# The first three weight chunks as plain fp32 products, issued between the modulation sums

## The reference, cut to what matters

```python
c_act = jax.nn.silu(c)
mod = (c_act @ w_ada[l] + b_ada[l])[:, None, :]
sh1, sc1, g1, sh2, sc2, g2 = jnp.split(mod, 6, axis=-1)
h = _rmsnorm(x, norm_g[l, 0]) * (1.0 + sc1) + sh1
...
z = h @ w_in            # qa, ka, va, qb, kb, vb, fb, qc, kc, vc, qi, ki, wi, zg
...
qc_r = _rope(heads(qc, C_HEADS), cos, sin)
kc_r = _rope(kc[:, :, None, :], cos, sin)[:, :, 0, :]
qi_r = _rope(heads(qi, IDX_HEADS), cos, sin) * (IDX_DIM ** -0.5)
ki_r = _rope(ki[:, :, None, :], cos, sin)[:, :, 0, :]
```

## Time and profile before

| | |
|---|---|
| median of 3 runs | 810.53 us (810.25 to 810.9) |
| the profiled execution's own time | 810.55 us |
| its span, first to last instruction | 808.8 us |
| mean granted TensorE clock | 0.972 of full speed |
| TensorE busy | 752.6 us, 93% |
| VectorE busy | 538.7 us, 67% |
| ScalarE busy | 397.1 us, 49% |
| GpSimd busy | 108.3 us, 13% |

### The profile page before, as it was taken

How to read it: one execution, slowest core, us unless ns; L and a number is a source line. 1 busy time by engine, 2 the same in 40 slices (tenths; PEclk the granted TensorE clock), 3 DMA queues, 4 the chain that set the end, 5 groups by cost and what they waited for, 6 DMA issues and landing times. The chain is left out here.

```text
span 808.8 us, 14361 instructions
## 1 busy us (share of the span) xinstructions
PE 752.6 (93%) x6052; PEld 734.9 (91%) x6052; DVE 538.7 (67%) x776; ACT 397.1 (49%) x540; POOL 108.3 (13%) x91
## 2 busy tenths in 40 slices
PE   2499999999897999999999999999999999999995
PEld 2499999999896999999999999999989999999994
DVE  4968988666856677777746456926675556566554
ACT  3175555555424554444443337618445565655533
POOL 0020000000500100000000060000005754342000
PEclk9699999999998999999999999969999999999998
DMA  9965555655345165545565614523335644334001
GB/s 353 415 237 194 222 207 216 245 203 214 115 145 220 53 209 208 185 181 186 202 244 202 213 56 168 201 101 103 122 141 184 207 171 157 105 105 158 1 1 53
DMA packets 20952, 139.57 MB, mean 173 GB/s; under 512 B 2356, under 2 KB 2996, under 8 KB 5016
## 3 DMA queue, kind: packets, MB, share of 16 engines
q1 hardware_dynamic: 20600, 137.80, 47.2%
q0 software_dynamic: 288, 0.85, 0.3%
HBM read 137.59 MB, written 1.05 MB: 171 GB/s over the span
## 5 line engine op out<-in xcount | busy, mean ns | idle before, releaser
L941 DVE TENSOR_TENSOR wlo<-raw,whi 128x2048 fp32r<-128x2048 f32 (+1 forms) x106 | 239.1, 2257 | 156.8 <-ACT whi L584 152.2
L1463 PE MATMUL res<-hhi,whi 128*128 128x256 f32 (+1 forms) x1168 | 337.1, 289 | 6.3 <-DVE hlo L977 4.2
L1464 PE MATMUL res<-hhi,wlo 128*128 128x256 f32 (+1 forms) x1168 | 331.3, 284 | 0.0
L1465 PE MATMUL res<-hlo,whi 128*128 128x256 f32 (+1 forms) x1168 | 331.3, 284 | 0.0
L584 ACT ACTIVATE whi<-raw 128x2048 fp32r<-128x2048 f32 (+1 forms) x106 | 197.7, 1867 | 154.1 <-issue 115.7
L1463 PEld LDWEIGHTS res<-hhi,whi 128*128 128x128 f32 (+1 forms) x1168 | 223.6, 191 | 8.6 <-issue 3.8
L1464 PEld LDWEIGHTS res<-hhi,wlo 128*128 128x128 f32 (+1 forms) x1168 | 223.6, 191 | 0.3
L1465 PEld LDWEIGHTS res<-hlo,whi 128*128 128x128 f32 (+1 forms) x1168 | 223.4, 191 | 0.2
L1463 PE MATMUL res<-uhi,whi 128*128 128x256 f32 x176 | 50.0, 284 | 1.0 <-ACT y L778 1.0
L1464 PE MATMUL res<-uhi,wlo 128*128 128x256 f32 x176 | 49.4, 281 | 0.0
L1465 PE MATMUL res<-ulo,whi 128*128 128x256 f32 x176 | 49.4, 281 | 0.0
(11 more groups left out here) (293 smaller groups left out, 1164.9 us busy)
## 6 DMA issues: line engine op xcount, KB each, us to landing
raw<-in_wts SPq DMA_DIRECT2D x100, 1024.0 KB, 5.0
raw<-in_w_ada SPq DMA_DIRECT2D x16, 1024.0 KB, 6.1
gates<-in_w_ada SPq DMA_DIRECT2D x6, 1024.0 KB, 8.2
raw<-in_wts SPq DMA_DIRECT2D x4, 768.0 KB, 7.6
y<-in_w_ada SPq DMA_DIRECT2D x2, 1024.0 KB, 10.7
x<-in_xT SPq DMA_DIRECT2D x2, 512.0 KB, 6.3
outT<-x SPq DMA_DIRECT2D x4, 256.0 KB, 2.4
biasA<-in_relb SPq DMA_DIRECT2D x1, 768.0 KB
```

Of the source, the lines that this page charges most:

```text
L941: nc.vector.tensor_tensor(wlo[c % SPL][:, 0:b], raw[RAW_OF["w", c] % RAW][:, 0:b], whi[c % SPL][:, 0:b].bitcast(f32), ALU.subtract).then_i ...
L1463: mm(out, ah, bh, start=first, stop=False)
L1464: mm(out, al, bh, start=False, stop=False)
L1465: return mm(out, ah, bl, start=False, stop=last)
```

## The change

The chunks 0 to 2 (`DIRECT = 3`) are no longer split. They are loaded whole into the place of `gates`, and `direct(c, j)` multiplies them in fp32 by the tiles `tb`, two input tiles (a pair j) at a time, four matmuls a call. The modulation blocks lie in three new shared buffers and `y`. ScalarE makes `tb` (scale and shift in one instruction) from `x` times the root, which VectorE puts into `sq` for all pairs at once (`rooted`). `c` arrives as one row of 4 KB and TensorE spreads it with two fp32 matmuls of one contraction row and 512 columns. The constants for mixer C move behind chunk 4 in SyncE's order and wait there for all eight modulation blocks. `MISC` becomes the first chunk that is split. Some semaphores are merged, and `warm` may use `meanw` instead of `ident`.

```diff
+STREAM = []
+for _i in range(4):
+    STREAM += [("ada", _i), ("ada", 4 + _i)] + [("w", _i)] * (_i < DIRECT)
 for _c in range(NC):
-    if _c:
+    if _c >= DIRECT:
         STREAM.append(("w", _c))
...
         def _(sp):
-            sp.dma_start(cact[:, :], crow_d).then_inc(c_in, 16)
+            sp.dma_start(crow, crow_d).then_inc(c_in, 16)
...
-                        if i == 2:
+                        if i == 7:
                             sp.dma_start(ident[:, :], ident_d).then_inc(ident_in, 16)
+                            sp.dma_start(rope1[:, :, :], rope1_d).then_inc(ident_in, 16)
                         continue
-                if (kind, n) == ("w", 1):
-                    for dst, src in ((rope1[:, :, :], rope1_d), (amask[:, :], amask_d), (cmask[:, :], cmask_d),
+                if kind == "w" and n < DIRECT:
...
+                    sp.dma_start(direct_weights(n).rearrange("p a b -> p (a b)"), src).then_inc(direct_full[n], 16)
+                    continue
+                if (kind, n) == ("w", 5):
+                    sp.wait_ge(ada_used, 2 * 8)
+                    for dst, src in ((amask[:, :], amask_d), (cmask[:, :], cmask_d),
                                      (sel[:, :], sel_d), (biasA[:, :, :], rel_d)):
                         sp.dma_start(dst, src).then_inc(mixc_in, 16)
...
-            act.wait_ge(c_in, 16)
-            nc.scalar.activation(cact[:, :], cact[:, :], ACT.Silu).then_inc(c_ready, 1)
-            act.wait_ge(const_in, 16)
-            load_root()
+            for i in range(2):
+                act.wait_ge(c_spread, i + 1)
+                nc.scalar.activation(cact[:, 512 * i:512 * i + 512], pT[:, 512 * i:512 * i + 512], ACT.Silu, scale=float(D)
+                                     ).then_inc(c_ready, 1)
             act.wait_ge(x_in, 32)
             for k in range(KT):
                 nc.scalar.activation(sq[:, k, :], x[:, k, :], ACT.Square).then_inc(squares["n1"], 1)
+            act.wait_ge(const_in, 16)
+            load_root()
             norm_guess("n1", "eps6")
-            split_hi("n1", tb, lambda k: mod[:, k:k + 1], range(6))
-            high(0)
-            split_hi("n1", tb, lambda k: mod[:, k:k + 1], range(6, KT))
-            for c in range(1, SPL):
-                high(c)
+            for j in range(4):
+                act.wait_ge(xr_ready, j + 1)
+                act.wait_ge(ada_used, ada_done(j))
+                act.wait_ge(pcol_ready, j + 1)
+                for k in (2 * j, 2 * j + 1):
+                    nc.scalar.activation(tb[:, k, :], sq[:, k, :], ACT.Identity, bias=mod[:, k:k + 1],
+                                         scale=pcol[:, 0, k:k + 1]).then_inc(scaled["n1"], 1)
+                split_hi("n1", tb, None, (2 * j, 2 * j + 1))
+            high(DIRECT)
+            high(DIRECT + 1)
...
                 if b <= KK:
                     swap(b, 32)
+                    if b == QC:
+                        high(c + 4)
...
+            def scale_columns(j):
+                dve.wait_ge(ada_used, ada_done(4 + j))
+                nc.vector.scalar_tensor_tensor(pcol[:, 0, 2 * j:2 * j + 2], mod[:, 8 + 2 * j:10 + 2 * j], 1.0,
+                                               col("norm_g", 2 * j, 2), ALU.add, ALU.mult).then_inc(pcol_ready, 1)
+            def rooted(j):
+                nc.vector.tensor_tensor(sq[:, 2 * j:2 * j + 2, :], x[:, 2 * j:2 * j + 2, :],
+                                        rstd[:, None, :].to_broadcast([P, 2, T]), ALU.mult).then_inc(xr_ready, 1)
+            dve.wait_ge(c_ready, 2)
+            ada(0)
+            norm_rstd("n1")
+            ada(4)
+            scale_columns(0)
             for j in range(4):
+                rooted(j)
+            for j in range(1, 4):
                 ada(j)
-                if j == 3:
-                    low(0)
+                split_lo("n1", tb, None, (2 * j - 2, 2 * j - 1))
                 ada(4 + j)
...
+                scale_columns(j)
+            low(DIRECT)
+            split_lo("n1", tb, None, (6, 7))
+            low(DIRECT + 1)
...
+            def direct(c, j):
+                pe.wait_ge(direct_full[c], 16)
+                for k in (2 * j, 2 * j + 1):
+                    pe.wait_ge(scaled["n1"], k + 1)
+                    for i in range(2):
+                        last = mm(res[c][:, i * T:i * T + T], direct_weights(c)[:, k, i * P:i * P + P], tb[:, k, :],
+                                  start=i == 0 and k == 0, stop=i == 1 and k == KT - 1)
+                if j == 3:
+                    last.then_inc(product_done, 1)
+            pe.wait_ge(c_in, 16)
+            for i in range(2):
+                mm(pT[:, 512 * i:512 * i + 512], meanw[0:1, :], crow[:, 512 * i:512 * i + 512], start=True, stop=True
+                   ).then_inc(c_spread, 1)
+            warm(12, meanw)
             mean("n1", sq, range(KT), squares["n1"], KT)
-            pe.wait_ge(ident_in, 16)
-            pe.wait_ge(ada_used, ada_done(6))
-            warm(20)
-            for c in range(NC):
+            warm(16, meanw)
+            for c, j in ((QC, 0), (QI, 0), (QC, 1), (QI, 1), (KK, 0), (KK, 1), (QC, 2), (QI, 2), (KK, 2), (QC, 3), (QI, 3), (KK, 3)):
+                direct(c, j)
+                if j == 0 and c < KK:
+                    warm(8, meanw)
+            for c in range(DIRECT, NC):
                 if c < BRANCH:
-                    if c == QC:
-                        fm(c, hhi, hlo, None, lambda k: pe.wait_ge(in_lo["n1"], k + 1), range(KT))
-                    elif c == MISC:
+                    if c == MISC:
+                        pe.wait_ge(in_lo["n1"], KT)
```

More of the change, by code:

```diff
@@ L138 @@
         STREAM.append(("ada", ADA_AFTER[_c]))
-RING = [e for e in STREAM if e[0] == "w" or e[1] >= 8]
+RING = [(kind, n) for kind, n in STREAM if n >= (DIRECT if kind == "w" else 8)]
 RAW_OF = {e: i for i, e in enumerate(RING)}
@@ L342, in build @@
         ada_used = sem("ada_used")
-        c_in, ident_in = sem("c_in"), sem("ident_in")
+        direct_full = [sem(f"direct_full{i}") for i in range(DIRECT)]
+        c_in, ident_in, c_spread = sem("c_in"), sem("ident_in"), sem("c_spread")
+        xr_ready, pcol_ready = sem("xr_ready"), sem("pcol_ready")
         x_in, const_in, mixc_in, glac_in, swac_in = (sem(n) for n in ("x_in", "const_in", "mixc_in", "glac_in", "swac_in"))
@@ L642, in _ @@
                     nc.scalar.activation(alrT[:, :], ps[0:16, 0:T], ACT.Copy).then_inc(drained_act, 1)
-                if b not in LATE:
+                if b not in LATE and b >= DIRECT:
                     high(c + 2)
@@ L958, in norm_rstd @@
             def norm_rstd(n):
-                dve.wait_ge(guess_known[n], 1)
+                dve.wait_ge(guess_known, NORMS.index(n) + 1)
                 if n in centered:
@@ L1123, in _ @@
                                                  ).then_inc(fcum_ready, 1)
-                if b not in LATE and not GOUT <= b < SK and not b >= SOUT and not (b in RH and b > KK):
+                if b not in LATE and not b < DIRECT and not GOUT <= b < SK and not b >= SOUT and not (b in RH and b > KK):
                     low(c + 2)
                 if b == QC:
-                    dve.wait_ge(mixc_in, 80)
+                    dve.wait_ge(ident_in, 32)
                 if b <= KK:
                     rope(b, (qkv["qc"][:, :, :], qkv["qi"][:, :, :], kroped)[b], rope1)
+                if b == QC:
+                    low(c + 4)
                 if b == MISC:
+                    own(nc.vector.memset(fones, 1.0))
+                    dve.wait_ge(mixc_in, 64)
                     for h in range(4):
@@ L1507, in fm, with warm @@
                         half()
-            def warm(n):
+            def warm(n, of=ident):
                 for _ in range(n):
-                    mm(pS[:, 512:640], ident[:, :], ident[:, :], start=True, stop=True)
+                    mm(pS[:, 512:640], of[:, :], of[:, :], start=True, stop=True)
             def fm_first(c, ih, il, ready, order=range(KT)):
```

70 lines of the change are left out of this document (31 added, 39 removed).

## The result

| | before | after |
|---|---|---|
| median | 810.68 us (4 runs, 810.25 to 810.9) | 804.83 us (4 runs, 804.23 to 805.16) |
| ratio | | 0.9928, 95% interval 0.991 to 0.9945 |
| profiled execution, its span | 810.55, 808.8 us | 805.16, 803.4 us |
| mean granted TensorE clock | 0.972 | 0.978 |

What follows compares the result with a forecast made beforehand. TensorE is busy 93% of the span; VectorE bounds the start, and ScalarE's chain holds back TensorE's restart. 810.55 - 6.0 (earlier restart) + 1.5 (clock's fall) = 806.0 us, own range 805 to 807.3.

Steps and rivals of the forecast that it cites:

- root refined: Start: VectorE refines the root until 16.0 us, up to 1 us later if the clock rises later.
- last scale column: End of VectorE's modulation sums: column 3 at 39.3 us, against 39.8 before.
- `QC`, `KK` done: TensorE's direct products: `QC` done at 41.3 us, `KK` at 44.7, against 57.1 for `KK` before.
- chunk 5 usable: SyncE's stream: `high(5)`'s chunk, behind 1.14 MiB of constants issued at 39.1, lands at 46.6 us.
- `MISC` copy: ScalarE's copy at the end of its swaps and uppers, before the transposes: at 57.6 us.
- mark moved by: Mark is TensorE's restart with `QA`'s upper half, behind the `MISC` transposes: from 64.24 to 58.2, 6.0 us earlier.
- clock's fall at the restart: TensorE's clock falls to 0.50 after the idle gaps; half speed loses 1.0 to 1.7 us, taken as 1.5.
- later stages: Everything behind the mark keeps its order on each engine, so the gain stays: 0 us.
- Rival (b): SyncE's wait for all eight sums makes chunk 5 and what follows 2 to 3 us late: 808.5 us; chance 0.10.
- Rival (a): TensorE's clock holds through the gaps: 804.5 us; chance 0.22.
- (c): Slower: direct products run at the low clock, `QC` ends at 54.9, mark 4.7 us late: 815 us; chance 0.06.
- (d): Gain absorbed later, as another engine sets the pace up to the `ZG` chunks: 810.5 us; chance 0.04.

Runs made afterwards that it cites:

- the control: The kernel after, unchanged, run again on the chip of a later series; 806.3 us, ratio 0.994 to the kernel before.
- after_sums: Kernel after, but all twelve direct calls wait for the last `tb` tile and run chunk by chunk; 818.21 us, ratio 1.0083 to the kernel before.
- gap_uppers: Kernel after with mixer C's constants ahead of chunk 7 and `high(6)`, `low(6)` moved behind the swap of `QI`; 800.18 us, ratio 0.9863.
- c_by_dma: Kernel after, but `c` loaded as 128 equal rows, 512 KB, and not spread by TensorE; 805.76 us, ratio 0.993.
- consts_late: Kernel after with mixer C's constants and SyncE's wait moved from ahead of chunk 5 to ahead of chunk 7; 804.99 us, ratio 0.9925.
- uppers_again: Same program as gap_uppers, run once more in another series; 803.34 us, ratio 0.9893.
- late_and_warm: consts_late plus 6 warm matmuls before `QA` and 12 before the `MISC` transposes; 802.24 us, ratio 0.9888.

## Why the prediction was right

| step | forecast | measured |
|---|---|---|
| block 0 lands | 10.3 | 9.86 |
| root refined | 16.0 | 16.11 |
| last scale column | 39.3 | 38.57 |
| `QC`, `KK` done | 41.3, 44.7 | 42.5 (estimated: 28.84 + 8 x 1.71), 46.27 |
| chunk 5 usable | 46.6 | 48.33 |
| `MISC` copy | 57.6 | 59.32 |
| mark moved by | 6.0 | 4.34 |
| clock's fall at the restart | 1.5 | 0 here, 1.5 in the control |
| later stages | 0 | +1.04 |
| time (profiled execution) | 806.0 | 805.16 |

The mechanism was right in the main: the sums' end moves little (39.8 to 38.57), 12 us are offered by the direct products (57.1 to 46.3 is 10.8), ScalarE's chain takes more than half of that (6.5), and the gain stays behind the mark. `after_sums` shows the first cause, `gap_uppers` the second.

That the sum came within 0.8 us is in part luck. The mark moved 1.7 us less than summed, the clock's fall cost 1.5 less, and later stages gave 1.04 that was not in the sum: 810.55 - 4.34 - 1.04 = 805.17. The clock's 1.5 us and the mark's 1.7 cancel nearly to nothing, and in the control, where the clock did cost 1.5 behind the restart, the profiled execution took 806.8 us.

**The term that was mis-sized is chunk 5.** I had 4.6 us and 2.57 us a MiB for 1.14 MiB of constants, with SyncE's wait released at 39.1. It was released earlier, at 38.56, and the chunk still came 1.7 us later than summed. The queue ran empty behind chunk 4 and the refill was slow: 74 GB/s in 39 to 40, 339, 141, 334 and 365 in the four us behind. Three of these windows (the last two numbers are the DMA engines' share and GB/s):

```profile
39.00:40.00 1.00, 1.00 (x6) 0.90 (x5) 0.00 (x0) 1.00 (x3) 0.89 (x3) 1.00 0.34 74
...
41.00:42.00 1.00, 1.00 (x6) 0.88 (x5) 0.84 (x2) 1.00 (x2) 0.94 (x3) 1.00 0.57 141
...
43.00:44.00 1.00, 1.00 (x7) 0.87 (x6) 1.00 (x1) 0.97 (x2) 0.58 (x3) 1.00 0.98 365
```

The sum had 408 GB/s for all of it. In the window with 141 GB/s the engines were busy only 0.57 of the time. The DMA view of 36 to 50 counts 356 of 887 packets under 2 KB, but that the short packets of the masks made the refill slow isn't shown. Nor is the refill all of it. A chunk lands in sixteen parts, and in the trace's landing records of the kernel after those of chunk 5 came between 46.10 and 48.31, half of them by 46.41, two tenths ahead of the forecast; the last one set the time. In `c_by_dma`, which issued the constants 1.07 us later, the sixteen came between 47.57 and 48.23. So the first part lands later when the issue is later, and the spread up to the last one differs between the two executions (0.7 us here, 2.2 there). How the 1.7 us is shared between the slow refill and this spread isn't shown. Rival (b) had the late chunk, at 0.10, by the queue that starts empty; its place and sign were right and its size, 2 to 3 us, a little high.

**`QC` was late by 1.2 us** because the eight calls up to its end began at 28.84, not at 27.6. The first direct call took 3.3 us, from 20.23 to 23.54, instead of 1.7, as the granted clock was 0.50 from 19.9 to 23.3; in the control it was 1.00 there, the call took 1.8 us and the eight calls began at 27.46. It cost nothing here, as ScalarE was not ready before 42.95; in `consts_late` it held the swap for 0.49 us.

**The clock** fell as forecast, but in 54 to 57.5, where TensorE had slack, since `QA`'s lower half began late (53.64, with the bank of `QI` free only then and not at 51.8). That half ran at 0.50 and used up most of the pause, so TensorE's longest wait is the one for the bank, 4.3 us, and not the one for the copy, 1.5, as the prediction's signs have it. The forecast put the fall's cost behind the restart, which is right for the control and for `consts_late`; its own remark that a fall inside the gaps costs nothing is right for the kernel after. Rival (a), that the clock holds, is out, though its 804.5 us is nearest to the median. The Trainium skill, page "TensorE: Matmul & The Clock Gate", section "HAM oscillation — how this bites in real kernels", says that pauses between bursts throttle the clock; these traces agree (0.50 in 54 to 56 behind a pause of 4.3 us). In `gap_uppers`, whose three pauses here are 1.1 to 1.7 us, the clock stayed at 1.00. Only the place of a fall decided its price.

**Later stages** gave 1.04 us that I had at zero. All profiled kernels gained between the drain and the end, 0.5 to 2.9 us, mostly at 238 to 260 and at 530 to 540 us, in stretches with a granted clock of 0.50. The time at 0.50 between the drain and 790 us bears this out in part: it adds up to 23.9 us before, and to 13.7 in `consts_late` and `uppers_again`, which gained 2.3 and 2.7 us, against 20.5 in the six kernels that gained 0.5 to 1.4. But the kernel after and `late_and_warm` have 23.9 us too and gained 1.0 and 1.7, so the clock is not the whole cause. All gains are against one profiled execution of the kernel before, and a loss of its own would show as a gain of all; this stays open. Rivals (c) and (d) are out: the clock was 1.00 from 24 to 54, and the offset is there at the end.

## What to carry to other kernels

When products are laid beside the work that produces their input, price what stands behind them next: here a serial chain on ScalarE took 6.5 of the 10.8 us, and five changed lines that filled two of its pauses gave another 2 to 6. Warm-up matmuls in front of work that others wait for delay it (twelve of them, 4.6 us long, brought the root 1.8 us later here), so put them only where TensorE would idle with nobody waiting. And price a DMA queue that is let run empty by more than its bytes: here the chunk behind the empty queue was usable 1.7 us later than bytes at the full rate gave. When several terms of a sum err by over 1 us each, a total that fits is no proof of them; compare term by term.

## What the runs showed of the hardware

In one execution of the program TensorE's clock fell once in this stretch, at 54.0 (over by 57.4); in another execution of the same program it fell at 53.4 (over by 56.8) and again at 60.2, with a difference of 1.5 us at one place. An edit under 2 us on TensorE's path is therefore read at the offsets of single instructions, not at the median of a few runs. The start shows a second thing: the windows have 1.00 as the clock there, but ScalarE received the results of the two spreading matmuls 1.71 us apart (4.47 and 6.18). That is, for 512 columns and one contraction row, twice the steady 0.427 us per 256 columns. The first means of the kernel before are alike: their records up to 12.7 us have a median of 634 ns, those of the earlier trace rows 379. By this the engine ran at half speed there, as at 1.2 GHz, though no row says so.
